# Attention with two softmax maps: another order of work within a head, other places for v's copies and the norm, slopes moved into q

## What is computed

```python
def diff_attention(q, k, v, lam, slopes):
    # q, k (b,s,h,2,d) with d = 64; v (b,s,h,128); 8 heads, s = 1024
    scores = einsum("bqhrd,bshrd->bhrqs", qi, k) * d ** -0.5
    scores = scores - slopes[h] * abs(q_pos - k_pos)      # slopes[h] = 2 ** -(h + 1)
    probs = softmax(scores)
    w = probs[:, :, 0] - lam * probs[:, :, 1]
    return einsum("bhqs,bshe->bqhe", w, v)
...
o = rms_norm(o, subln_g) * (1.0 - lam_init)
y_attn = o * silu(g)
```

## Time and profile before

| | us |
|---|---|
| median of 3 runs | 4300.45 (4299.6 to 4301.29) |
| the profiled execution | 4300.27 |
| its span, first to last instruction | 4298.5 |
| PE busy | 3813.0, 89% |
| VectorE busy | 2173.9, 51% |
| ScalarE busy | 1659.5, 39% |
| mean granted clock of PE | 0.947 |

### The profile page before, as it was taken

The page is one execution under the profiler, slowest core; times in us unless marked ns, Lnnn a source line. Parts: engine busy times, 40 slices in busy tenths (PEclk is TensorE's granted clock), DMA queues, the critical chain, the costliest instruction groups (busy, mean ns, idle before and its releaser), DMA issues.

```text
span 4298.5 us, 48819 instructions
## 1 busy us (share of the span) xinstructions
PE 3813.0 (89%) x20470; PEld 3150.6 (73%) x20470; DVE 2173.9 (51%) x2809; ACT 1659.5 (39%) x2219; POOL 528.7 (12%) x437
## 2 busy tenths in 40 slices
PE   6989999999988999788888877999888899879988
PEld 5768978788766777666666646977777777658988
DVE  3444243443464667355444552367777877732222
ACT  4323222112135556466656551144444444431122
POOL 0000011001011435000000000012222222200002
PEclk9989999999998999899999988999999999989999
DMA  2002011111111010100000004121111111142111
GB/s 87 30 25 79 30 64 50 49 49 45 44 60 40 30 48 12 49 25 25 25 25 25 27 15 159 40 79 30 40 40 40 35 50 45 47 179 79 40 40 64
DMA packets 196398, 211.31 MB, mean 49 GB/s; under 512 B 7943, under 2 KB 171732, under 8 KB 196180
## 3 DMA queue, kind: packets, MB, share of 16 engines
q1 hardware_dynamic: 190420, 187.22, 13.7%
q10 hardware_dynamic: 5760, 20.97, 1.3%
HBM read 174.62 MB, written 33.55 MB: 48 GB/s over the span
## 4 chain that ended last, share of the span: by engine, by line
PE 66%; DVE 16%; ACT 11%; issue 5%; DMA 2%; POOL 0%; SPq 0%; ACTq 0%; DVEq 0%; POOLq 0%
PE pd L211 56%; PE pq L211 7%; ACT t L2340 2%; DVE t L2392 2%; ACT t L311 2%; PE pd L354 2%; DVE t L320 2%; DVE t L2714 1%; PE pq L354 1%; DVE t L3117 1%; DVE t L2706 1%; DVE t L1785 1%; DVE t L2410 0%; DVE t L3102 0%; ACT L2376 0%
## 5 line engine op out<-in xcount | busy, mean ns | idle before, releaser
L211 PE MATMUL pd<-t 128*128 128x512 f32 (+2 forms) x15920 | 3128.0, 357 | 137.4 <-DVE t L599 43.4
L211 PEld LDWEIGHTS pd<-t 128*128 128x128 f32 x15920 | 2580.0, 193 | 625.4 <-issue 169.9
L211 PE MATMUL pq<-t 128*128 128x128 f32 (+5 forms) x3222 | 570.7, 339 | 133.5 <-DVE t L2392 37.9
L211 PEld LDWEIGHTS pq<-t 128*128 128x128 f32 (+2 forms) x3222 | 398.4, 185 | 262.8 <-DVE t L2392 58.3
L311 ACT ACTIVATE t<-t 128x2048 fp32r<-128x2048 f32 (+2 forms) x134 | 241.6, 1804 | 753.8 <-PE pd L211 696.4
L320 DVE TENSOR_TENSOR t<-t 128x2048 fp32r<-128x2048 f32 (+2 forms) x134 | 296.0, 2210 | 370.2 <-ACT t L311 370.2
L354 PE MATMUL pd<-t 128*128 128x128 f32 x832 | 139.7, 322 | 120.9 <-DVE t L2410 32.4
L1385 DVE TENSOR_TENSOR t<-pd,t 128x512 f32<-128x512 f32 x256 | 171.7, 689 | 122.9 <-PE pd L211 122.9
L354 PEld LDWEIGHTS pd<-t 128*128 128x128 f32 x832 | 118.4, 168 | 147.3 <-ACT t L2221 35.0
L2340 ACT ACTIVATE t<-t 128x1024 f32<-128x1024 f32 x128 | 146.2, 1144 | 94.1 <-DVE t L2397 94.1
L2714 DVE SCALAR_TENSOR_TENSOR t<-t 128x1024 f32<-128x1024 f32 x120 | 178.6, 1489 | 0.3
(11 more groups left out here) (284 smaller groups left out, 2808.8 us busy)
## 6 DMA issues: line engine op xcount, KB each, us to landing
t<-in_w_in_dram SPq DMA_DIRECT2D x97, 512.0 KB, 5.1
t<-in_w_mlp_dram SPq DMA_DIRECT2D x32, 1024.0 KB, 5.3
t<-in_w_out_dram SPq DMA_DIRECT2D x20, 1024.0 KB, 5.1
t<-in_w_in_dram SPq DMA_DIRECT2D x16, 1024.0 KB, 5.3
t<-ym_scratch ACTq DMA_DIRECT2D x24, 512.0 KB, 8.5
t<-in_x_dram SPq DMA_DIRECT2D x16, 512.0 KB, 7.2
x_scratch<-t SPq DMA_DIRECT2D x16, 512.0 KB, 2.8
ym_scratch<-t SPq DMA_DIRECT2D x16, 512.0 KB, 2.6
```

The source lines that it names most:

```text
L211: ins = e.matmul(out, l, r, start=(first and j == 0), stop=(last and j == n - 1), skip_group_check=True)
```

## The change

Five things, all within the attention stage.

- The bias stays minus the distance, made once in the setup. q is multiplied by 2^(h-2) where it is split, and the reduction scales scores and bias by 2^-(h+1).
- The norm of an AV half (`pe_att_ms` and its like: norm product, Ln, Exp, y, store) no longer follows AV. The first half's is done at tile 5 (PE, ScalarE) and 6 (VectorE, SP), the second's at tiles 1 and 2 of the next head. ScalarE squares before it copies.
- v's two copies and transposes are steps of their own: both v blocks come first, then their copies, and each v transpose stands before a g block.
- On ScalarE the weight unit is a step ahead of k's and q's outputs, which come one step later.
- `tmp` has four buffers, and a line of letters in `att_stage` gives the order in place of `weave` (a a step of attention, d one of v and g).

```diff
@@ rings and setup
-    tmp = ring(ph, 2, [128, 512])
+    tmp = ring(ph, 4, [128, 512])
+        e.mul(bias[:, :], bias[:, :], -1.0).then_inc(*at.inc("act", "bias"))
@@ def pe_att_vg
         for th in range(2):
             if h:
                 fm(e, u, 0, th, 2, "av", h, th)
             yield
+        yield
+        for th in range(2):
             b = e.take(PD, "avT", h, th)
...
-            yield
-        for th in range(2):
             if h:
                 fm(e, u, 128, th, 2, "ag", h, th)
+                if th == 1:
+                    pe_done(u)
+            yield
+            yield
@@ def act_att_qk, def dve_att_qk (q's part)
+                e.mul(QS[0][LO, sl], b[LO, :], 2.0 ** (h - 2)).then_inc(*at.inc("act", "qk0", h, m, th))
+                e.mul(QS[1][HI, sl], b[HI, :], 2.0 ** (h - 2)).then_inc(*at.inc("act", "qkh", h, m, th))
...
+                e.scalar_tensor_tensor(QS[0][HI, sl], b[LO, :], 2.0 ** (h - 2), QS[0][LO, sl].bitcast(F32), MUL,
+                                       SUB).then_inc(*at.inc("dve", "ql0", h, m, th))
@@ the norm
+    def owed(h, tt):
+        return (h, 0) if tt >= 4 else (h - 1, 1)
+
+    def pe_att_ms(e, h, tt):
+        h, th = owed(h, tt)
+        if h >= 0:
+            b = e.take(PD, "oms", h, th)
+            e.wait_ge(*at["osq", h, th])
+            mms(e, b[:, :], [(ones[:, :], tmp.of("osq", h, th)[:, :])]).then_inc(*at.inc("pe", "oms", h, th))
+
+    def act_att_ms(e, h, tt):
+        h, th = owed(h, tt)
+        if h >= 0:
+            q = tmp.of("osq", h, th)
+            e.wait_ge(*at["oms", h, th])
+            e.wait_ge(*at["epsc"])
+            e.activation(q[:, :], PD.of("oms", h, th)[:, :], ACT.Ln, scale=1.0 / 128, bias=epsc[:, 0:1]).then_inc(
+                *at.inc("act", "oln", h, th, free=("oms", h, th)))
+            e.wait_ge(*at["oln", h, th])
+            e.activation(q[:, :], q[:, :], ACT.Exp, scale=-0.5).then_inc(*at.inc("act", "ors", h, th))
@@ def pe_att
             if tt < 6:
                 scores(tt + 2)
+            if tt in (1, 5):
+                pe_att_ms(e, h, tt)
...
-                b = e.take(PD, "oms", h, th)
-                e.wait_ge(*at["osq", h, th])
-                mms(e, b[:, :], [(ones[:, :], tmp.of("osq", h, th)[:, :])]).then_inc(*at.inc("pe", "oms", h, th))
@@ def act_att
-        e.mul(bias[:, :], bias[:, :], -4.0 if h == 0 else 0.5).then_inc(*at.inc("act", "bias", h))
...
                 *at.inc("act", "wTc", h, tt, 0, free=("wT", h, tt, 0)))
+            if tt in (1, 5):
+                act_att_ms(e, h, tt)
             yield
...
-                e.copy(o[:, :], b[:, :]).then_inc(*at.inc("act", "o", h, th))
-                e.activation(q[:, :], b[:, :], ACT.Square).then_inc(*at.inc("act", "osq", h, th, free=("AV", h, th)))
...
+                e.activation(q[:, :], b[:, :], ACT.Square).then_inc(*at.inc("act", "osq", h, th))
+                e.copy(o[:, :], b[:, :]).then_inc(*at.inc("act", "o", h, th, free=("AV", h, th)))
@@ def dve_att
                 *at.inc("dve", "wTc", h, tt, 1, free=("wT", h, tt, 1)))
+            if tt in (2, 6):
+                dve_att_ms(e, h, tt)
             yield
@@ def att_stage
         for h in range(8):
+            a = att(e, h)
             if h < 7:
-                a = att(e, h)
                 d = vg(e, h + 1)
-                next(a)
-                next(d)
-                weave((islice(a, 18), 18), (d, 5))
+                for who in "dada" "adaa" "aaa" "adaa" "aadaa" "adada" "a":
+                    next(a if who == "a" else d, None)
                 weave((a, 9), (qk(e, h + 1), 4))
             else:
-                steps(att(e, h))
+                steps(a)
+        ms(e, 8, 0)
```

More of the change, by code:

```diff
@@ L2184, in act_att_setup @@
         e.wait_ge(*at["dist"])
-        e.activation(bias[:, :], bias[:, :], ACT.Abs).then_inc(*at.inc("act", "bias", -1))
+        e.activation(bias[:, :], bias[:, :], ACT.Abs).then_inc(*at.inc("act", "abs_dist"))
+        e.wait_ge(*at["abs_dist"])
+        e.mul(bias[:, :], bias[:, :], -1.0).then_inc(*at.inc("act", "bias"))
     def pe_att_first(e):
@@ L2235, in act_att_vg @@
                 *at.inc("act", "agt", h, th, free=("ag", h, th)))
-            yield
+            if th == 0:
+                yield
+    QK4 = [(1, 0), (1, 1), (0, 0), (0, 1)]
     def pe_att_qk(e, h):
         u = pe_unit(e, W2in, [(2592 + h * 128, 128), (3616 + h * 128, 128)])
[L2240 to L2244, removed]
-    def act_att_qk(e, h):
-        act_unit(e)
[L2248 to L2260, removed]
@@ new lines, in pe_att_qk, with out_ @@
+        for m, th in QK4:
+            fm(e, u, m * 128, th, 2, "aqk", h, m, th)
+            if (m, th) == QK4[3]:
+                pe_done(u)
+            yield
+    def act_att_qk(e, h):
+        def out_(m, th):
+            sl, b = half(th), PD.of("aqk", h, m, th)
+            e.wait_ge(*at["aqk", h, m, th])
+            if h:
+                e.wait_ge(*at["scores", h - 1, 7, 1])
+            if m == 0:
+                e.mul(QS[0][LO, sl], b[LO, :], 2.0 ** (h - 2)).then_inc(*at.inc("act", "qk0", h, m, th))
+                e.mul(QS[1][HI, sl], b[HI, :], 2.0 ** (h - 2)).then_inc(*at.inc("act", "qkh", h, m, th))
+            else:
+                e.copy(KS[0][LO, sl], b[LO, :]).then_inc(*at.inc("act", "qk0", h, m, th))
+                e.copy(KS[1][HI, sl], b[HI, :]).then_inc(*at.inc("act", "qkh", h, m, th))
+                e.copy(KS[0][HI, sl], b[LO, :]).then_inc(*at.inc("act", "kc", h, th))
+                e.copy(KS[1][LO, sl], b[HI, :]).then_inc(*at.inc("act", "qkh", h, m, th))
+            at.also("act", ("aqk", h, m, th))
+        act_unit(e)
+        yield
+        for i in range(4):
+            out_(*QK4[i])
+            if i < 3:
@@ new lines, in dve_att_qk @@
+        dve_unit(e)
+        yield
+        for i in range(4):
+            out_(*QK4[i])
+            if i < 3:
+                yield
+    def owed(h, tt):
[16 more added lines that the diff above has]
+            e.activation(q[:, :], q[:, :], ACT.Exp, scale=-0.5).then_inc(*at.inc("act", "ors", h, th))
@@ new lines, in dve_att_ms @@
+    def dve_att_ms(e, h, tt):
+        h, th = owed(h, tt)
+        if h >= 0:
+            gs = AB[h % 2][0][:, half(th)]
+            e.wait_ge(*at["o", h, th])
+            e.wait_ge(*at["agt", h, 0])
+            e.wait_ge(*at["agt", h, 1])
+            e.scalar_tensor_tensor(gs, tmp.of("o", h, th)[:, :], pc("subln"), gs, MUL, MUL).then_inc(
+                *at.inc("dve", "og", h, th, free=("o", h, th)))
+            e.wait_ge(*at["og", h, th])
+            e.wait_ge(*at["ors", h, th])
+            e.tensor_tensor(gs, gs, tmp.of("osq", h, th)[:, :], MUL).then_inc(
+                *at.inc("dve", "oy", h, th, free=("osq", h, th)))
@@ L2280, in pe_att, with sp_att_ms @@
+    def sp_att_ms(e, h, tt):
+        h, th = owed(h, tt)
+        if h >= 0:
+            r = (8 + h) * 128
+            e.wait_ge(*at["oy", h, th])
+            e.dma(YM[r:r + 128, half(th)], AB[h % 2][0][:, half(th)], "ya", h, th)
     def pe_att(e, h):
@@ L2388, in scores @@
             x = e.take(sm, "x", h, tt)
-            e.wait_ge(*at["bias", h])
+            e.wait_ge(*at["bias"])
             for r in range(2):
```

70 lines of the change are left out of this document (23 added, 47 removed).

## The result

| | us | ratio to before | 95% interval |
|---|---|---|---|
| before, median of 4 runs | 4300.02 (4296.41 to 4301.29) | | |
| changed, median of 4 runs | 4393.18 (4383.87 to 4394.3) | 1.0213 | 1.0196 to 1.0231 |
| changed, the profiled execution | 4383.87, span 4382.1 | | |

The change makes the kernel 93 us slower. The profiled execution is the quickest of the four: its mean granted clock is 0.941, that of the others 0.937.

What follows compares the result with a forecast made beforehand. PE was taken to bound heads 0 to 6, by work plus idle time and slow clock. Heads 1 to 6 +98, head 0 +10, head 7 -2 summed to +106: span 4404, time 4405 us, own range 4375 to 4430.

Steps and rivals of the forecast that it cites:

- (a) to (f): Attention stage: bias scaling, squares' waits (2 x 1.17) and v copy's wait (2.66) go, weight split earlier; slopes, y's DMA 0.
- (a): Bias no longer scaled per head: 8 x 1.80 us of ScalarE go, one 1.80 comes in the setup, +-0.5 there.
- (b): Slope in q's scale: four half-width operations a head change by between -0.05 and +0.1 us each; taken as 0.
- (g): Ring of four PSUM buffers: PE waits until the fourth product before was read; 6.4, 6.8, 2.3, 3.3 us in middle heads.
- k block with slow clock to 98.5: Middle head's second k block: after a 3.3 us wait for Ln it runs at slow clock, ending at t = 98.5.
- the walk: Step-by-step timing of one middle head from the end of the previous AV, t = 0, to its own AV's end, 118.7 us.
- the prediction's check: Middle head by terms: 84.5 work + 27.4 idle + 6.7 clock = 118.6 us.
- Head 7: No projections: norm at tile 1 costs 2.6, removed work gives 3 and 5.5, norm at tile 5 costs 4: -2 us.
- The clock rival: Attention heads: waits come as walked but PE keeps its clock; heads 1 to 6 take 112.0 us, total 4362; chance 0.19.
- Buffers don't bind: Attention heads: the ring is miscounted, Ln and Silu stand in nobody's way; 108.3 us a head, total 4340; chance 0.08.
- Faster: Attention heads: no buffer waits, and the softmax chain runs ahead of PE; 96.5 us a head, total 4259; chance 0.08.
- Longer loads: ScalarE's table loads on the path each cost 1.2 us more; 5 x 1.2 x 7 heads, total 4447; chance 0.02.

Runs made afterwards that it cites:

- e10: Kernel before with only the slopes taken into q, all steps in their old order: 4284.1 us, ratio to before 0.9963.
- e1: Changed kernel, but VectorE copies the norm product from PSUM to SBUF and Ln reads the copy: 4350.2 us, ratio to before 1.0121.
- e9: Changed kernel with norm back behind AV, Silu of half 0 before tile 4's exps, g block of half 1 ahead of AV: 4309.6 us.
- e4: Changed kernel with the norm put back behind AV on all engines: 4350.9 us, ratio to before 1.0121.
- e2: Changed kernel with Silu of half 0 moved ahead of tile 4's exps: 4414.0 us, ratio to before 1.0268.
- e6: Changed kernel with repeated transposes on PE filling idle time ahead of the two long waits: 4372.5 us, ratio to before 1.0171.
- e8: Changed kernel's parts in a new order: first scores before first v block, Silu early, norms at tiles 0 and 4, VectorE copying half 0's norm product: 4195.7 us.
- e3b: Changed kernel with second v transposes and g block of half 1 ahead of AV of half 0: 4377.6 us, ratio to before 1.0177.

## Why the prediction was right, and where its sizes were off

The forecast of 4405 was 12 us above the median, which its own range of 4375 to 4430 held, and the mechanism is the one it named. By its terms, in the profiled execution (us against before):

| term | predicted | measured |
|---|---|---|
| head 0 | +10 | +10.2 (108.5 against 98.3) |
| heads 1 to 6 | 6 x 16.4 = 98 | 6 x 13.7 = 82.2 (period 116.05 against 102.35) |
| head 7 | -2 | -4.4 (77.6 against 82.0) |
| outside these windows | 0 | -4.4 |
| span | +106 | +83.6 |

**Removed waits, (a) to (f).** Right in the changed kernel: squares and v's copy cost PE nothing there. (a) and (b) by themselves bring 17 us (e10), about half of it by way of the clock, a gain that the sum had in no term. In the setup (a) had +-0.5; in the changed kernel the blocks ahead of head 0 start 1.5 us later (1775.45 against 1773.93), which stands in the window of head 0.

**The ring, (g).** Right, with its places. Predicted against measured in head 4: 6.4 and 6.20 for Ln, 2.5 and 1.82 for mixing, 6.8 and 6.35 for Silu, 2.3 and 2.10 for Silu of half 1, 3.3 and 2.80 for Ln again. AV of half 0 started at 57.1 (57.2 predicted) and lasted 9.64 (9.4). That a buffer causes the first of these waits is shown by e1; that Silu causes the third, by e9, and that it comes without the norm's move, by e4.

**The step that was mis-sized** is "k block with slow clock to 98.5". Up to the end of AV of half 0 the walk is off by 0.2 us (66.8 against 66.6), and part of that is luck: PE is idle for 19.0 us there and not for the walk's 20.9 (small gaps 3.3 for 4.5, and each of the long ones a little shorter), while the g block takes 8.58 and not 7.6, since its clock stays at 0.50 for 6 us and not for 4. The first k block ends at 86.9 (86.8). The second starts at 90.6, walked as 91.1, and takes 5.73 and not 7.4: after 2.80 us of idleness PE kept its full clock. With 0.4 us in the rest this gives 116.05 in place of 118.7, six times 2.65, 16 us. I had taken the slow clock of this block from the earlier trace rows, where 2.94 us of idleness brought it. In e1, e2 and e6 k blocks behind 2.1 us took 7.3.

By the terms of the prediction's check, PE is idle for 24.4 of 116.05 us where it had 27.4, and busy 7.2 above the 84.5 of work where it had 6.7 for the clock: as a whole the slow clock was sized well, by two errors that nearly cancel, and the idle time was 3 us too long. That a slow clock behind those waits also makes the other three executions of the changed kernel 9 us longer than the profiled one fits their lower clock, but only one execution has a trace, so it is argued, not shown.

**Head 0** came out at +10.2 against +10 by luck. Its AV of half 0 starts at 49.4 and not at 47.1, 1.5 of it from ahead of the window, and what follows AV takes 49.4 and not 52.1.

**Head 7** gained 4.4 and not 2: up to the end of its first AV it gained 1.2 us (47.0 against 48.2) where the terms had 0.4, behind it 3.2 (30.6 against 33.8) where they had 1.5. In both halves the AV product itself was quicker, 8.92 for 9.42 and 9.06 for 9.85; no run parts that from the norm's place. **Outside the windows** the work is unchanged; behind the stage it took 1701.3 us against 1705.7. Of these 4.4, 3.4 lie in one stretch of a later stage: the same 184 matmul records take 47.87 us before (2822.69 to 2870.56) at a mean granted clock of 0.86, and 44.43 after (2910.29 to 2954.72) at 0.96. So it is the clock again; why it differs there no run shows.

**The rivals.** The clock rival (4362) fell: the blocks took 8.58 and 9.64, with a clock of 0.50 over the first 6.0 us of one and the first 5.0 of the other. It was right about the second k block alone. e6 fills two of the three idle times and gained 21 us of some 34, since slow clock moved elsewhere; the 43 between rival and forecast it doesn't test. "Buffers don't bind" fell with e1. "Faster" (4259) needs a softmax chain ahead of PE, and this order has none. e8 went below even that time, 4195.7, by another way: its reductions still stand 5.3 us apart where tiles follow each other, as in the earlier trace rows, but PE has projections over the chain wherever it would wait. Longer loads (4447) fell: between load and activation stand 10 ns at Ln (2286.52 to 2286.53) and at Silu (2309.50 to 2309.51), and ahead of Ln's load 20 ns (the copy there ends at 2285.22). The Trainium skill, page ScalarE: Activation LUTs, section What ACT_TABLE_LOAD costs, would have a drain of about 1.38 us there; the trace does not agree, and the measurement decides.

## What to carry to other kernels

Where several engines' outputs share a ring of PSUM buffers, write down who comes fourth before whom after every change of order, and when each is read: the reader that frees a buffer last (here Ln and Silu behind exps) is a wait of PE that no line of the change shows. Do it again for each repair: two of mine (e2, e9) met the next such dependence, a store and the same ring. If the late reader can't move, let an idle engine copy the buffer out, which was worth 43 us here, and judge an order by the whole period of a head, since a move that is a draw in one order (+4 us) cost 42 in another.

## What the runs showed of the hardware that I had not expected

PE's clock after two to three us of idleness isn't a matter of their length alone. A block of 24 matmuls took 5.72 behind 2.10 us and 5.73 behind 2.80 in every head of the changed kernel, but 7.3 behind 2.1 in all seven heads of e1; transposes with the block behind them took 1.94 and 6.51 behind 2.94 before, 1.06 and 5.72 behind 2.92 in e10. A program keeps its pattern from head to head (the changed kernel, e1) or turns between two of them (e2, e3b), and a small edit elsewhere switches it, by 1.6 to 2.5 us a head: more than several of the terms that a prediction adds up. The fall of the clock need not lie in the idle time either. In head 4 of e1 the k block starts at 2311.90 at a granted clock of 1.00; it falls to 0.50 at about 2312.7, with PE busy, and is back at 1.00 at about 2316.2. Ahead of the g block of the changed kernel it falls at about 2283.1, 2 us after PE's last transposes. Behind 6.2 us the block was slow in each head (8.6 in the changed kernel, 8.46 in e3b, 7.10 at the least in e2); with repeated transposes in the gap and 2.71 us of it left (e6), it took 5.76.
